# Two rounds of four: modulation products placed in halves among the steps of four attentions

## What is computed

```
for l in range(2):
    sh1, sc1, g1, sh2, sc2, g2 = split(silu(c) @ w_ada[l] + b_ada[l])     # c: 1024, w_ada[l]: 1024 x 6144
    h = rmsnorm(x, norm1_g[l]) * (1 + sc1) + sh1
    A = differential attention (4 heads, two maps of 64 each)
    B = pooling over windows;  C = attention with a sink and a +-128 window (8 heads of 64)
    x = x + g1 * (sum of sigmoid gates * branch projections of A, B, C) @ w_out[l]
    h2 = rmsnorm(x, norm2_g[l]) * (1 + sc2) + sh2
    x = x + g2 * channel_mixer(h2)      # dense for l = 0, top 2 of 8 experts for l = 1
```

## Time and profile before

| | us |
|---|---|
| three runs: median (lowest to highest) | 1478.9 (1478.65 to 1479.46) |
| the profiled execution, its own time | 1479.42 |
| its span in the profile | 1477.7 |
| PE matmul busy | 1445.6 |
| VectorE busy | 907.6 |
| ScalarE busy | 729.4 |
| first attention, from its scores 2 to the next stage | 194.14 to 220.99 |
| second | 275.58 to 307.71 |
| third | 841.00 to 866.54 |
| fourth | 921.13 to 952.39 |

### The profile page before, as it was taken

One profiled execution on the slowest core, in us unless ns is written; L12 is line 12 of the kernel. 1 busy time (PEld: TensorE's weight loads), 2 busy tenths in 40 slices (PEclk: granted clock), 3 DMA queues, 4 the chain that ended last, 5 costly groups with the idle time before them and its releaser, 6 DMA issues.

```text
span 1477.7 us, 22390 instructions
## 1 busy us (share of the span) xinstructions
PE 1445.6 (98%) x8951; PEld 1276.5 (86%) x8951; DVE 907.6 (61%) x1081; ACT 729.4 (49%) x867; POOL 59.7 (4%) x59
## 2 busy tenths in 40 slices
PE   7999999999999999999999999999999999999997
PEld 5788969789999999998889879699888888888884
DVE  4543266555644345427532373737899999989888
ACT  4433354453433233225434262733478787787754
POOL 0100000000000000001000000001200000000030
PEclk9999999999999999999999999999999999999999
DMA  9844365468763355263532271645599999999991
GB/s 325 287 162 165 114 209 183 130 203 276 235 198 108 115 143 142 95 233 125 172 126 86 94 244 62 215 156 194 172 390 395 390 391 394 391 388 383 350 330 65
DMA packets 229146, 326.48 MB, mean 221 GB/s; under 512 B 8485, under 2 KB 154822, under 8 KB 228798
## 3 DMA queue, kind: packets, MB, share of 16 engines
q1 hardware_dynamic: 220160, 296.02, 58.7%
q0 software_dynamic: 6832, 25.88, 5.0%
q10 hardware_dynamic: 2062, 3.24, 0.6%
HBM read 310.14 MB, written 14.97 MB: 220 GB/s over the span
## 4 chain that ended last, share of the span: by engine, by line
PE 91%; DVE 4%; DMA 2%; ACT 1%; issue 1%; ACTq 0%; POOL 0%; DVEq 0%; SPq 0%; POOLq 0%
PE ps L766 26%; PE ps L768 25%; PE ps L767 25%; PE ps L783 2%; PE ps L1004 2%; PE ps L1038 1%; PE ps L1022 1%; DMA mrows<-g2d 1%; DMA raw<-in_w_ex_down_dram 1%; PE ps L859 1%; PE ps L1326 1%; PE ps L1286 1%; PE ps L983 0%; ACT ebuf L1721 0%; PE ps L793 0%
## 5 line engine op out<-in xcount | busy, mean ns | idle before, releaser
L766 PE MATMUL ps<-hhi,whi 128*128 128x384 f32 x824 | 277.0, 336 | 0.3 <-DVE hidlo L2659 0.3
L768 PE MATMUL ps<-hhi,wlo 128*128 128x384 f32 x824 | 275.7, 335 | 0.0
L767 PE MATMUL ps<-hlo,whi 128*128 128x384 f32 x824 | 275.7, 335 | 0.0
L2047 DVE TENSOR_TENSOR wlo<-raw,whi 128x2048 fp32r<-128x2048 f32 x65 | 148.7, 2289 | 173.7 <-ACT whi L1549 161.6
L766 PEld LDWEIGHTS ps<-hhi,whi 128*128 128x128 f32 x824 | 154.8, 188 | 2.6 <-issue 2.0
L767 PEld LDWEIGHTS ps<-hlo,whi 128*128 128x128 f32 x824 | 154.8, 188 | 0.3
L768 PEld LDWEIGHTS ps<-hhi,wlo 128*128 128x128 f32 x824 | 154.8, 188 | 0.0
L2538 DVE TENSOR_TENSOR wlo<-mraw,whi 128x2048 fp32r<-128x2048 f32 (+2 forms) x72 | 143.5, 1993 | 14.4 <-ACT whi L1818 14.0
L2538 DVE TENSOR_TENSOR wlo<-raw,whi 128x2048 fp32r<-128x2048 f32 (+2 forms) x72 | 144.3, 2019 | 11.9 <-ACT whi L1818 11.6
L1549 ACT ACTIVATE whi<-raw 128x2048 fp32r<-128x2048 f32 x60 | 114.6, 1912 | 74.0 <-PE ps L768 58.9
L1818 ACT ACTIVATE whi<-mraw 128x2048 fp32r<-128x2048 f32 (+2 forms) x72 | 120.9, 1679 | 57.1 <-PE ps L768 54.7
(11 more groups left out here) (422 smaller groups left out, 2500.2 us busy)
## 6 DMA issues: line engine op xcount, KB each, us to landing
raw<-in_w_ada_dram SPq DMA_DIRECT2D x62, 512.0 KB, 5.3
raw<-in_w_gate_dram SPq DMA_DIRECT2D x48, 512.0 KB, 4.6
raw<-in_w_ex_up_dram SPq DMA_DIRECT2D x24, 1024.0 KB, 8.9
raw<-in_w_ex_down_dram SPq DMA_DIRECT2D x24, 1024.0 KB, 8.4
raw<-in_w_in_dram SPq DMA_DIRECT2D x43, 512.0 KB, 5.7
raw<-in_w_ex_gate_dram SPq DMA_DIRECT2D x16, 1024.0 KB, 8.1
mraw<-in_w_ex_gate_dram SPq DMA_DIRECT2D x16, 1024.0 KB
mraw<-in_w_ex_down_dram SPq DMA_DIRECT2D x16, 1024.0 KB, 9.4
```

The source lines that it names most:

```text
L766: pe.matmul(out, s[0], m[0], start=first, stop=False, **kw)
L767: pe.matmul(out, s[0], m[1], start=False, stop=False, **kw)
L768: return pe.matmul(out, s[1], m[0], start=False, stop=last, **kw)
L2047: dve.tensor_tensor(wlo[:, n % RING, :], raw[:, n % RING, :], whi[:, n % RING, :].bitcast(F32), ALU.subtract).then_inc(lo_done, 1)
```

## The change

`ADA_STEPS` becomes `ADA_HALVES`. A product is cut in two rounds, k = 0 to 3 and k = 4 to 7, and the table says at which step each round stands (round n belongs to product 2 + n // 2 of the phase). If a step has two rounds listed, the first stands before its transposes and the others behind them, ahead of values t - 1. `mm_done` counts up after the second round. Products 0 and 1 stay whole and where they were.

```
-ADA_STEPS = {2: (1, 3, 5, 7, 9, 10), 3: (1, 4, 6, 8, 10), 4: (1, 4, 6, 9), 5: (1, 4, 6, 9)}
+ADA_HALVES = {2: (0, 1, 1, 3, 4, 4, 6, 7, 7, 9, 10, 10), 3: (1, 1, 3, 4, 4, 6, 7, 7, 10, 10),
+              4: (1, 1, 4, 4, 7, 7, 10, 10), 5: (1, 1, 4, 4, 7, 7, 10, 10)}
...
-            def ada_product(phase, i):
+            def ada_product(phase, i, ks=range(KD)):
...
-                for k in range(KD):
+                for k in ks:
...
-                mm.then_inc(mm_done, 1)
+                if ks[-1] == KD - 1:
+                    mm.then_inc(mm_done, 1)
...
+                def ada_half(n):
+                    ada_product(phase, 2 + n // 2, range(4 * (n % 2), 4 * (n % 2) + 4))
...
-                    if t in ADA_STEPS[phase]:
-                        ada_product(phase, 2 + ADA_STEPS[phase].index(t))
+                    halves = [n for n, step in enumerate(ADA_HALVES[phase]) if step == t]
+                    if halves:
+                        ada_half(halves[0])
                     transposes(t)
+                    for n in halves[1:]:
+                        ada_half(n)
```

More of the change, by code:

```diff
@@ L79 @@
 GROUPS = ADA_SLOTS[0] // 2
-ADA_STEPS = {2: (1, 3, 5, 7, 9, 10), 3: (1, 4, 6, 8, 10), 4: (1, 4, 6, 9), 5: (1, 4, 6, 9)}
-assert all(2 + len(ADA_STEPS[p]) == ADA_SLOTS[p] <= 16 for p in ADA_STEPS)
+ADA_HALVES = {2: (0, 1, 1, 3, 4, 4, 6, 7, 7, 9, 10, 10), 3: (1, 1, 3, 4, 4, 6, 7, 7, 10, 10), 4: (1, 1, 4, 4, 7, 7, 10, 10), 5: (1, 1, 4, 4, 7, 7, 10, 10)}
+assert all(4 + len(ADA_HALVES[p]) == 2 * ADA_SLOTS[p] <= 32 and max(ADA_HALVES[p]) < 11 for p in ADA_HALVES)
 SQS = (0, 1, 1 + N_HALF, 2 + N_HALF)
```

## The result

The changed kernel took 1485.39 us (median of 6 runs, 1483.62 to 1486.45), the kernel before 1479.14 (median of 6): 6.25 us more, a ratio of 1.0041 with a 95% interval of 1.0031 to 1.0051. Slower was the likeliest side of the forecast, but the time lies 3.2 us above the forecast of 1482.2 and above the end of its range.

What follows compares the result with a forecast made beforehand. TensorE, busy for almost the whole span, was taken as the bound. Attention terms 3.0 - 0.4 + 0.5 + 0.1 gave +3.2 to 3.3 us, so 1482.2 us against the median; range 1480.0 to 1484.8, the forecast's own 1481.0 to 1483.4.

Steps and rivals of the forecast that it cites:

- The stall: First attention, step 1: PE waits 2.6 us before the fourth product's first round until its slot's load lands.
- the clock falls in the stall: Rival: clock falls to 1.2 GHz in the first attention's idle stretch, 1.8 us lost, 1484.0 us; chance 0.03.
- First attention: Layer 0's differential attention: +3.0 us, from the wait for the fourth product's slot, nine rounds and the remaining work.
- Second: Layer 0's windowed attention: +0.70 us of added work, waits 1.9 to 0.7, together -0.4 us.
- Third: Layer 1's differential attention: eight rounds +0.56 us, four behind transposes +0.36, waits 1.5 to 1.05, together +0.5.
- Fourth: Layer 1's windowed attention: +0.56 us of work, waits 2.0 to 1.5, together +0.1.
- the upper bound of 0.65: Highest cost considered for one round, in us, if leaving to a values group also costs 0.09; 0.57 was taken.
- the waits at step 10: Attentions two to four: with one round ahead instead of a product, waits grow to 0.6 or 0.7 us.
- rounds are cheaper: Rival: a round costs 0.50 us and nothing for following transposes; +1.6 us, 1480.5 us; chance 0.15.
- the slot lands later: Rival: first attention's half-load takes 6.6 us, not 4.6; +1.9 us more, 1484.1 us; chance 0.11.
- all waits vanish: Rival: rounds around transposes keep PE from ever waiting in attentions two to four; sum -3.5 us, 1475.4; chance 0.06.
- The stall isn't there: Rival: first attention's slot is filled in time after all; +0.9 us, 1479.8 us; chance 0.03.

Runs made afterwards that it cites:

- whole product early: Kernel before with only the first attention's fourth product put, whole, behind step 1's transposes, no rounds; 1484.91 us, ratio 1.0035 to the kernel before.
- cut in place: Kernel before with products at their old steps, each cut in two rounds around its step's transposes; 1482.72 us, ratio 1.0023 to the kernel before.
- whole moved: Kernel before with whole products moved to other steps in all four attentions, meant never ahead of their slot; 1479.18 us, ratio 1.0000.
- three moved: Kernel before with whole products moved in the second to fourth attention, the first in its old order; 1477.49 us, ratio 0.9986.
- the changed kernel again: The changed kernel rerun with no edit; 1485.67 us, ratio 1.0037 to the kernel before.
- first whole: Changed kernel with the first attention back to whole products at the old steps, the other three in rounds; 1480.51 us, ratio 1.0006 to the kernel before.
- filled: Changed kernel with 11 identity matmuls, result unread, put into the first attention's stall; 1482.38 us, ratio 1.0020 to the kernel before.
- no wait: Changed kernel with the first attention's rounds at later steps so none comes before its slot has landed; 1481.56 us, ratio 1.0014 to the kernel before.
- part filled: Changed kernel with 5 identity matmuls put into the first attention's stall; 1482.36 us, ratio 1.0023 to the kernel before.

## Why the prediction was wrong

**Which step failed.** The stall was found, with its place, its cause and its size (2.6 forecast, 2.55 to 3.05 in the profiles). What failed is the rival "the clock falls in the stall": the sum took the clock as whole, and the rival had a chance of 0.03 and a price of 1.8 us. Even with it the time would have been 1484.0, 1.4 us short. It fell in every profile in which PE was left idle there for 2.5 us or more (the changed kernel twice, the whole product early), stayed whole in the two where the stall was filled in part or in full, and cost 1.7 us where it stayed down for 3.41 us and more where it was 6.83. By medians it is 3.3 us, about the 3.2 between the forecast and the result. The mean granted clock of the whole program, on record for every execution, extends this beyond the profiles, though it can't say where the clock fell: it was 0.994 to 0.996 in all 11 executions of the changed kernel and all 5 of the whole product early, and at least 0.997 in 20 of the 22 with the stall filled and in 50 of 68 of the kernel before.

**Why it was set so low.** I took one idle stretch of the same length, at 1046.7 before the router, with the clock whole in the windows of one execution, as evidence that such a stretch does nothing. In the other executions the same place goes both ways. After idle stretches of 1.80, 1.74, 1.95, 2.65 and 1.80 us there the clock fell just behind (the changed kernel, cut in place, whole moved, whole early, three moved), after 2.15, 1.89, 1.39, 1.96 and 1.48 us it didn't (the changed kernel again, first whole, filled, no wait, part filled). PE's rows there in two of them, whole moved and no wait, with nearly the same idle stretch:

```profile
1047.50 0.41 PE L1244 MATMUL ps<-selz,slotc 128*128 128x32 f32 x2 [1.95 <-DVE selz L2369]
1048.44 3.64 PE L1216 MATMUL ps<-cst 128*128 128x128 f32 x16
```

```profile
1050.59 0.41 PE L1238 MATMUL ps<-selz,slotc 128*128 128x32 f32 x2 [1.96 <-DVE selz L2363]
1051.50 2.03 PE L1210 MATMUL ps<-cst 128*128 128x128 f32 x16
```

The same 16 matmuls take 3.64 us with the clock down and 2.03 with it whole. One draw of a thing that goes either way had been read as a rule.

**The terms.** First attention +3.0 forecast without the clock: the filled stall gives 30.17 - 26.85 = +3.3. Second -0.4: measured -0.3. Third +0.5: +0.8. Fourth +0.1: +0.3. So the sum without the clock was 3.3 forecast and 4.1 by these windows (3.4 and 3.0 by the medians of the two kernels with the stall filled; that these land where the forecast put the changed one is in part luck, since the windows show a term that was missed). The 0.8 missing seems mostly one term: I took a round behind transposes at 0.57 + 0.09 and let the values group behind it go free, though the upper bound of 0.65 had that step in it. A short values group takes 0.32 us to the next start behind transposes (198.77 to 199.09 in the timeline before) and 0.42 behind a round (202.39 to 202.81 in the filled kernel). Four such places in each differential attention make 0.4 each by this estimate, where the windows lack 0.3 each, and "cut in place" missed 0.4 each too. No run changed this term alone. The waits at steps 4 and 7 of the third attention were as forecast (from the round's start to the transposes 0.76 us, where a round alone takes 0.57).

**What held.** That nothing between the attentions takes up the loss; that the waits at step 10 grow by what the round is shorter than the product (0.71 against 0.72 forecast); that the 0.69 at step 5 of the second attention goes; that the later branch and gate loads of the fourth cost nothing. The wait at step 10 of the third attention is 0.61. Of the rivals, "rounds are cheaper" is refuted by the cut in place, "the slot lands later" accounts for 0.5 us in one profile and not for 3, and "all waits vanish" by the waits still there. "The stall isn't there" is what the no-wait kernel made true by its order: 1481.6, where the rival had 1479.8.

## To carry to other kernels

Before a piece of work is moved earlier in a queue, look up when its data lands, and count a stall of TensorE at its length plus what the clock may take behind it (here 1.7 us or more on a stall of 2.6); a few matmuls that compute nothing, put into a stall that can't be avoided, cost little and kept the clock here. Filler that is cut finer paid its start again with every piece here (0.16 us a product), so move it whole, and check who waits for the buffer that it holds for longer. A single execution that shows no clock fall after an idle stretch is one draw, not a bound.

## What was not expected of the hardware

- The same idle stretch brought the clock down for 3.41 us in one execution and for 6.83 in another, though PE was busy for 6.59 of these. In the latter the clock was down 0.2 us before PE went on.
- An idle stretch of 1.74 us before the router was followed by the lower clock, and one of 1.67 in the first attention wasn't; at the router stretches of 1.74 to 2.65 us were followed by it in five profiles and stretches of 1.39 to 2.49 us were not in six, so their length alone doesn't decide. What decides wasn't tried further; the work just ahead of and behind the stretch differs between the two places.
- The kernel's own order is near an edge: with the first attention unchanged, a slot load that landed in time in one execution held PE for 0.79 us in another.
